# Row products and sums on VectorE for the modulation vectors of a transformer kernel, in place of matmuls

## The reference

```
sc, sc_ctx = silu(c), silu(c_ctx)                      # two vectors of 1024
for l in range(2):
    mod   = split(sc     @ w_mod[l] + b_mod[l], 6)     # w_mod[l]: 1024 x 6144
    mod_x = split(sc_ctx @ w_mod[l] + b_mod[l], 6)
    sh1, sc1, g1, sh2, sc2, g2 = mod                   # each 1024
    h = layer_norm(x) * (1 + sc1) + sh1                # context likewise, with mod_x
    x = layer_norm(ALPHA * x + g1 * mixing(h)) * ln1_g[l] + ln1_b[l]
    x = layer_norm(ALPHA * x + g2 * swiglu(layer_norm(x) * (1 + sc2) + sh2)) * ln2_g[l] + ln2_b[l]
```

## Time and profile before

| | |
|---|---|
| median of 3 runs | 3742.49 us (3740.39 to 3747.37) |
| profiled execution | 3751.51 us, span of its instructions 3749.7 us |
| mean granted TensorE clock | 0.956 |
| busy: TensorE, VectorE, ScalarE, GpSimd | 92%, 38%, 36%, 13% of the span |
| modulation weights | 96 loads of 0.5 MB out of 283.85 MB in all |

### The profile page before, as it was taken

How to read it: one execution, slowest core, us unless ns; L and a number is a source line. 1 busy time by engine, 2 the same in 40 slices (tenths; PEclk the granted TensorE clock), 3 DMA queues, 4 the chain that set the end, 5 groups by cost and what they waited for, 6 DMA issues and landing times. The chain is left out here.

```text
span 3749.7 us, 62391 instructions
## 1 busy us (share of the span) xinstructions
PE 3444.4 (92%) x26194; PEld 3168.3 (84%) x26194; DVE 1414.6 (38%) x2382; ACT 1332.8 (36%) x2368; POOL 476.7 (13%) x462
## 2 busy tenths in 40 slices
PE   6999999989999899997988888999997899959997
PEld 5999997867678899996988767999995788849997
DVE  3223333444434422334345543222224436543333
ACT  3222322345533322234246534212224437452223
POOL 1000010144400010001013201101010103100000
PEclk9999999999999999998988988999998999979998
DMA  4333222110022233331200023221212310123231
GB/s 141 113 121 128 83 76 68 58 44 29 24 68 91 90 107 123 115 108 50 63 23 24 29 79 96 63 63 62 66 60 95 129 57 24 40 85 96 91 95 52
DMA packets 81556, 283.85 MB, mean 76 GB/s; under 512 B 8768, under 2 KB 13120, under 8 KB 81152
## 3 DMA queue, kind: packets, MB, share of 16 engines
q1 hardware_dynamic: 77584, 266.96, 21.9%
q0 software_dynamic: 3264, 12.37, 1.0%
q10 hardware_dynamic: 432, 0.53, 0.0%
HBM read 277.73 MB, written 2.10 MB: 75 GB/s over the span
## 5 line engine op out<-in xcount | busy, mean ns | idle before, releaser
L1981 DVE TENSOR_TENSOR r_Wbasel<-r_Wf,r_Wbaseh 128x1024 fp32r<-128x1024 f32 (+1 forms) x269 | 339.2, 1262 | 718.8 <-ACT r_Wbaseh L1438 718.3
L1438 ACT ACTIVATE r_Wbaseh<-r_Wf 128x1024 fp32r<-128x1024 f32 (+1 forms) x269 | 279.5, 1041 | 526.8 <-PE PS L926 466.3
L924 PE MATMUL PS<-r_X1h,r_Wbaseh 128*128 128x264 f32 (+2 forms) x1216 | 391.1, 322 | 28.6 <-DVE r_RS L2329 19.1
L926 PE MATMUL PS<-r_X1h,r_Wbasel 128*128 128x264 f32 (+2 forms) x1216 | 381.3, 314 | 0.0
L925 PE MATMUL PS<-r_X1l,r_Wbaseh 128*128 128x264 f32 (+2 forms) x1216 | 381.2, 314 | 0.0
L924 PE MATMUL PS<-r_X2h,r_Wbaseh 128*128 128x256 f32 (+1 forms) x1200 | 362.1, 302 | 11.6 <-DVE r_X2l L2107 5.5
L925 PE MATMUL PS<-r_X2l,r_Wbaseh 128*128 128x256 f32 (+1 forms) x1200 | 355.8, 297 | 0.0
L926 PE MATMUL PS<-r_X2h,r_Wbasel 128*128 128x256 f32 (+1 forms) x1200 | 355.4, 296 | 0.0
L924 PEld LDWEIGHTS PS<-r_X1h,r_Wbaseh 128*128 128x128 f32 x1216 | 233.8, 192 | 59.1 <-issue 23.4
L1981 DVE TENSOR_TENSOR r_Wtopl<-r_Wf,r_Wtoph 128x1024 fp32r<-128x1024 f32 (+1 forms) x140 | 171.2, 1223 | 261.4 <-ACT r_Wtoph L1438 261.2
L924 PE MATMUL PS<-r_X2h,r_Wtoph 128*128 128x256 f32 x880 | 248.7, 283 | 9.2 <-DVE r_Wtopl L1981 9.2
(11 more groups left out here) (361 smaller groups left out, 9237.3 us busy)
## 6 DMA issues: line engine op xcount, KB each, us to landing
r_Wf<-in_wmod SPq DMA_DIRECT2D x96, 512.0 KB, 3.6
r_Wf<-in_f_in SPq DMA_DIRECT2D x88, 512.0 KB, 3.7
r_Wf<-in_g_in SPq DMA_DIRECT2D x88, 512.0 KB, 3.5
r_Wf<-in_f_out SPq DMA_DIRECT2D x32, 448.0 KB, 3.2
r_Wf<-in_g_out SPq DMA_DIRECT2D x32, 448.0 KB, 3.2
r_Wf<-in_f_out SPq DMA_DIRECT2D x16, 512.0 KB, 4.1
r_Wf<-in_w_o SPq DMA_DIRECT2D x16, 512.0 KB, 3.5
r_Wf<-in_g_out SPq DMA_DIRECT2D x16, 512.0 KB, 3.5
```

Of the source, the lines that this page charges most:

```text
L924: self.e.matmul(o, wh, xh, start=first, stop=False)
L926: return self.e.matmul(o, wl, xh, start=False, stop=last)
L1438: e.activation(p.w(i, cols)[0], p.Wf[:, i % NW, 0:cols], ACT.Copy).then_inc(*p.hi.did(i))
L1981: e.tensor_tensor(l, p.Wf[:, i % NW, 0:cols], h.bitcast(F32), ALU.subtract).then_inc(*p.lo.did(i))
```

## The change

The modulation weights are laid out transposed, so that a tile holds 128 outputs as partitions and all 1024 inputs as columns: 48 tiles of 0.5 MB a layer. `c` and `c_ctx` are loaded as rows repeated on all partitions (two loads a layer on GpSimd's queue), ScalarE takes their Silu in place (the step `rows`), and for each tile VectorE makes two scalar_tensor_tensor instructions, weights times row, whose running sum is the modulation of that partition. Biases are added for eight tiles at once. The 48 steps `mod` of layer 0 are spread over the items of f1 and those of layer 1 over f2. The groups, their matmuls, their copies and their places in the planner are gone. SyncE, which waited for TensorE to free a raw tile's buffer, waits for VectorE.

```diff
+def mod_steps(l):
+    return [("rows", l)] + [("mod", l, m) for m in range(48)]
...
-def ffn_items(f, lag, gate, groups=()):
+def ffn_items(f, lag, gate, others=()):
...
-    firsts = [i for i, x in enumerate(items) if x[0][-1] == 0 and i > 12]
-    for n in reversed(groups):
-        i = firsts[len(firsts) * (groups.index(n) + 1) // (len(groups) + 2)]
-        items.insert(i + 2, (("mturn", n), 0.9, None))
-        items.insert(i + 1, (("msum", n), 1.8, None))
-    return items
+    out, n = [], 0
+    for i, x in enumerate(items):
+        out.append(x)
+        while n < len(others) and n * (len(items) - 24) < (i - 12) * len(others):
+            out.append((others[n], 0, None))
+            n += 1
+    return out
...
-    items = [(("open", "top", []), 0, None)] + ffn_items(f, 4, lambda c: c, [1, 2, 3, 4, 5])
+    items = [(("open", "top", []), 0, None)] + ffn_items(f, 4, lambda c: c, mod_steps(0))
...
-    return woven(items, chains, [(0, -1)])
+    return woven(items, chains)
...
-    items += ffn_items(f, 4, lambda c: c, [6, 7, 8, 9, 10])
+    items.append((("vectors", 1), 0, None))
+    items += ffn_items(f, 4, lambda c: c, mod_steps(1))
...
-        return woven(items, chains, [(n, ends[0]) for n in range(11, 16)] + [(n, ends[nc]) for n in range(16, 22)])
+        return woven(items, chains)
...
-    return woven(items, chains, [(n, ends[0]) for n in (22, 23)])
+    return woven(items, chains)
...  (TensorE: mod_sum and mod_turn removed; the step "mod" only counts the tile)
+        elif what == "mod":
+            self.finished(self.get("wmod", a, 1024, True))
...  (ScalarE: mod_copy and the Silu of c at the start removed)
+        elif what == "rows":
+            l, = a
+            e.wait_ge(*p.load(("c", l)).of("in"))
+            self.logs = False
+            for c in (0, 1):
+                e.activation(p.CR[l][c], p.CR[l][c], ACT.Silu).then_inc(*p.act.did(("rows", l, c)))
...  (VectorE)
+    def modulation(self, l, m):
+        p, e = self.p, self.e
+        u = self.get("wmod", (l, m), 1024, True)
+        w = p.Wf[:, u % NW, :]
+        e.wait_ge(*p.w_arrived(u))
+        if m == 0:
+            e.wait_ge(*p.act.of(("rows", l, 1)))
+        if m or l:
+            e.wait_ge(*p.dve.of(("first", l, m - 1) if m else ("first", l - 1, 47)))
+        e.scalar_tensor_tensor(p.JK[:, :], w, 1.0, p.CR[l][0], ALU.mult, ALU.mult, p.MOD[:, l, m, 0:1]).then_inc(
+            *p.dve.did(("first", l, m)))
+        e.scalar_tensor_tensor(w, w, 1.0, p.CR[l][1], ALU.mult, ALU.mult, p.MOD[:, l, m, 1:2]).then_inc(
+            *p.dve.did(("w", u), ("sum", l, m)))
+        self.finished(u)
+        if m % 8 < 7:
+            return
...  (bias for eight tiles: one instruction, or two where 1 / ALPHA is applied)
...  (GpSimd)
+        elif what == "vectors":
+            e.wait_ge(*p.mm.of(("mixout", 7, 1)))
+            self.vectors(*a)
...
+    def vectors(self, l):
+        p, e = self.p, self.e
+        for c in (0, 1):
+            e.dma_start(p.CR[l][c], p.A["c"][:, c, :]).then_inc(*p.load(("c", l)).did("in"))
...  (GpSimd's program)
+        for i in range(4):
+            e.wait_ge(*p.x_in[i].of("x"))
+        self.vectors(0)
         e.dma_start(p.H[:, :, T1:T1 + TC], p.A["ctx"]).then_inc(*p.ctx_in.did("x"))
...  (SyncE)
             if p.order[i - NW][3]:
-                e.wait_ge(*p.mm.of(("w", i - NW)))
+                e.wait_ge(*p.dve.of(("w", i - NW)))
...  (layout of the inputs)
-    a["wmod"] = np.ascontiguousarray(i["w_mod_2"].reshape(2, 2, 4, 128, 24, 256).transpose(0, 4, 1, 3, 2, 5)).reshape(
-        2, 24, 2, 128, 1024)
+    a["wmod"] = np.ascontiguousarray(i["w_mod_2"].transpose(0, 2, 1)).reshape(2, 48, 128, 1024)
+    c = np.stack([i["c_2"].reshape(-1), i["c_ctx_2"].reshape(-1)])
+    a["c"] = np.ascontiguousarray(np.broadcast_to(c[None], (128, 2, 1024)))
```

More of the change, by code:

```diff
@@ L36 @@
 NVEC = _n
-MODS = [(l, m) for l in range(2) for m in range(24)]
 GR = ((0, 384), (384, 640), (640, 1024))
@@ L604, in chain, with woven @@
     return out
-def woven(items, chains, groups):
-    t, pos, out, turns, groups = 0.0, 0, [], [], list(groups)
+def woven(items, chains):
+    t, pos, out = 0.0, 0, []
     at = [x[2] if x[1] is None else None for x in chains]
@@ L624, in woven @@
             continue
[L625 to L628, removed]
         gate = items[pos][2] if pos < len(items) else None
@@ L637, in woven @@
             continue
[L638 to L649, removed]
+        t = min(at[j] for j in range(len(chains)) if at[j] is not None and at[j] > t)
+    return out
 def last_of(items, kind, c, n):
@@ L709, in second_sequence @@
     chains += [(chain([a], c + 1), ends[2 + c], 0.8) for c in (0, 1)]
-    return woven(items, chains, [])
+    return woven(items, chains)
 def latent_sequence(p, l):
@@ L872, in partial_sum @@
         return n % 3, self.partial[n - 3] if n >= 3 else None
[L874 to L880, removed]
     def run(self, steps):
@@ L1078, in step @@
             self.tick(*a)
[L1080 to L1106, removed]
     def quarter_sums(self, b, src, g, n):
@@ L1490, in step @@
             self.apply(*a)
-        elif what == "msum":
-            self.mod_copy(*a)
+        elif what == "rows":
[4 more added lines that the diff above has]
+                e.activation(p.CR[l][c], p.CR[l][c], ACT.Silu).then_inc(*p.act.did(("rows", l, c)))
+        elif what == "mod":
+            self.finished(self.get("wmod", a, 1024, True))
         elif what == "bar":
@@ L1953, in program @@
         e.dma_start(p.CB[:, :, :], p.A["cb"]).then_inc(*p.const_in.did("all"))
[L1954 to L1957, removed]
         self.run(p.sequences[0])
@@ L2024, in step @@
             self.apply(*a)
[L2025 to L2028, removed]
+        elif what == "mod":
+            self.modulation(*a)
         elif what == "bar":
@@ L2055, in step @@
             self.tick(*a)
-    def mod_turn(self, n):
+    def modulation(self, l, m):
         p, e = self.p, self.e
[L2059 to L2063, removed]
-                            other).then_inc(*p.dve.did(("mod", l, m)))
+        u = self.get("wmod", (l, m), 1024, True)
[12 more added lines that the diff above has]
+            return
+        x = p.MOD[:, l, m - 7:m + 1, :]
+        b0 = VEC[f"bmod{l}"][0] + m - 7
+        b = p.V[:, b0:b0 + 8].unsqueeze(2).broadcast_to([128, 8, 2])
+        e.wait_ge(*p.dve.of(("sum", l, m)))
+        if m // 8 in (2, 5):
+            e.tensor_tensor(x, x, b, ALU.add).then_inc(*p.dve.did(("biased", l, m)))
+            e.wait_ge(*p.dve.of(("biased", l, m)))
+            e.tensor_scalar(x, x, 1.0 / ALPHA, None, ALU.mult).then_inc(*p.dve.did(("mod", l, m)))
+        else:
+            e.scalar_tensor_tensor(x, x, 1.0 if m // 8 in (1, 4) else 0.0, b, ALU.add, ALU.add).then_inc(
+                *p.dve.did(("mod", l, m)))
     def newton(self, x, y, t, ready, mul, key):
@@ L2964, in put @@
         v[:, s:s + n] = arr
-    pick = np.zeros((128, 2), np.float32)
-    for c in (0, 1):
-        pick[c::32, c] = 1.0
-    put("sum", pick)
     put("eps", np.broadcast_to(np.array(EPS, np.float32), (128, 4)))
```

33 lines of the change are left out of this document (9 added, 24 removed), and 4 rows, old and new, of the table _n.

## The result

| | before | after |
|---|---|---|
| median of timed runs, same chip | 3744.86 us (3740.39 to 3747.37) | 3681.59 us (3679.88 to 3687.85) |
| ratio, 95% interval | | 0.9835, 0.9818 to 0.9852 |
| profiled execution, its span | 3751.51, 3749.7 us | 3687.85, 3686.1 us |
| busy: TensorE, VectorE, ScalarE, GpSimd | 92, 38, 36, 13% | 92, 44, 36, 13% |

The change saves 63 us; the forecast was 3671.5 us, 71 us saved, with the range 3648 to 3706. The time lies in the range and 10 us above the forecast. (2.4 of the 10 are the kernel before: with a fourth run its median is 3744.9 us, and the forecast started from 3742.5.)

What follows compares the result with a forecast made beforehand. TensorE was taken to bound f1 and f2, a chain of small steps across engines the norm stretches. Savings of 38 - 3 + 30 + 6 = 71 us from 3742.5 gave 3671.5 us, range 3648 to 3706.

Steps and rivals of the forecast that it cites:

- Removed from f1 and f2: Feed-forward parts f1 and f2: ten groups leave TensorE's queue, 2.76 us each plus idleness ahead of L1104, saving 38 us.
- Short waits: f1 and f2: added VectorE sums sometimes delay other work, charged 3 us (0 to 15).
- 12 us of buffered work: f1 and f2: four buffers hold some 12 us of work, so one freed 6 us late still comes in time.
- The instruction: VectorE in f1 and f2: each scalar_tensor_tensor with running sum takes 1.38 us, 2.76 us a tile, 132 us a layer.
- end together: Earlier trace: GpSimd's subtraction of 2.41 us and VectorE's, begun 0.9 us later, were said to end together.
- Norm stretches: Second block's three norm stretches: without groups, sums and totals run earlier, saving 11, 9 and 10 us, together 30.
- rival 2: Norm stretches give all that the groups occupy, 45 us, and the start its 9: 3650 us; chance 0.10.
- Rival 1: Norm stretches give only 8 us because the ScalarE and VectorE chain sets their end: 3693.5 us; chance 0.12.
- The start: Kernel start: squares move up, but three splits in a row hold the feed-forward tiles; saves 6 us (1 to 9).
- Rival 3: f1 and f2: running sum halves VectorE's rate, 5.2 us a tile: 3758 us; loss from 5.0 us a tile; chance 0.09.
- Rival 4: f1 and f2: each modulation tile delays TensorE 0.5 us through late weights or buffers, 48 us: 3719 us; chance 0.09.

Runs made afterwards that it cites:

- e5: Kernel before without its groups 1 to 10 (those modulations set to 0.5, their weights not loaded): 3700.2 us, ratio 0.9881.
- e2: Kernel after with both sums of each modulation tile over 8 columns in place of 1024 (modulations then wrong): 3672.4 us, ratio 0.9802.
- e3: Kernel before with all 23 later groups in f1 (12) and f2 (11), none in the norm stretches: 3775.2 us, ratio 1.0079.
- e6: Kernel after with all activations 64 bytes further up on each partition: 3664.6 us.
- e4: Kernel after with the splits of the first four weight tiles ahead of the second chunk's norm: 3676.2 us, ratio 0.9812.
- e7: Kernel after with all activations 32 bytes further up, at a multiple of 512; total time not given.
- e8: Kernel after with activations 32 bytes further up and the top weight slots 480 bytes down; total time not given, 119.2 to 119.3 ns per matmul.
- e1: Kernel after with all activations 1088 bytes further up, as before the change, and the unread product JK as bf16; total time not given.
- e10: Kernel after with each sum made twice, four instructions of 1024 columns a tile: 3861.3 us, ratio 1.0307.

## Why the prediction came out right, and where its steps did not

1. **Removed from f1 and f2, 38 us.** Mis-sized: 52 by e5. The forecast counted the pieces and ScalarE's copies around one group, behind which the clock did not fall. Behind six of the ten it did, for some 10 of the missing 14 us; the rest of what a group costs, 3.9 to 4.6 us, is near the 3.8 of the forecast.
2. **Short waits, 3 us.** Mis-sized the other way: 13 by the traces of e2, within the 0 to 15 that the forecast allowed. They were put down to VectorE's order; but VectorE was idle ahead of every split that came late, and most of the delay is the turn of the buffers, which the forecast held for covered by 12 us of buffered work. It gave the higher traffic no price either; the feed-forward weights land at 4.4 us in place of 3.7. This alone costs little, as e2 has the same 4.4. 52 - 13 = 39 and the 40 that f1 and f2 gave agree; the forecast's 35 was near because two errors met.
3. **The instruction, 1.38 us.** Right: 1.22 and 1.37. The second of a pair is longer where GpSimd works: the one that began at 1502.48 took 1.76 us while GpSimd's subtraction ran from 1501.95 to 1503.16. So did all 26 second ones that met such a subtraction already under way (1.75 to 1.78); the 70 others took 1.21 to 1.23. Where the sum had begun ahead of the subtraction, as 26 first ones of a pair did, it kept its 1.22; one first sum began behind it and took 1.41. That fits the shared port of the Trainium skill ("SBUF — State Buffer", Who interferes with whom), which gives it to one engine at a time, and is small. (The prediction read in the earlier trace rows that two subtractions "end together"; by the rows they end at 51.44 and 52.51, so VectorE's ran on by itself for 1.07 us.)
4. **Norm stretches, 30 us.** 37.7 by e3, 38.6 in the change (of which 3 us are a shift within g0, which e3 and e6, with the old places, lose there too). Between the forecast and rival 2's 45. The third alone, 10, came as forecast; the first two give 4 us more each. TensorE's queue loses 25 and 23 us of work there; how that turns into 15 and 13 us, step by step, no run takes apart. Rival 1 (8 us) is out.
5. **The start, 6 us.** 8 us. The first matmul at 38.0, as forecast, and the splits of three tiles in a row.
6. **Missing: the places.** 15 us lost in g0 and g1 by the twins of e6 (7.3 and 7.7), 17 by the medians. The diff moves every activation by 1088 bytes, and the forecast gave that no term. This is the largest thing that it lacked. With the old distance back, e6 saves 82 us in its set (3746.2 - 3664.6), 11 more than forecast; the kernel after saves 8 less. The time lay in the range because these errors met, not because each term was right: that it is so near is luck.
7. **Missing, and no part of the change: 5 us between f1 and f2.** The time from the last matmul on H1 to the first on MX, the same work in all kernels, went from 772.7 (e4) to 780.2 us (e5), 775.3 before and 779.9 after. In all thirteen traces it follows the time that the clock spends at its lower level there: 13.7 us of it in e4 and e7 (772.7 and 773.0), 20.5 before and in e6 and e8 (775.3 to 775.7), 30.7 in e3, e5 and the kernel after (779.3 to 780.2). The same 23 matmuls, once in the kernel after, once in e4, show what differs, TensorE's granted clock:

```profile
978.00:982.50 4.50, 4.43 (x23) 3.93 (x23) 0.53 (x3) 0.01 (x1) 0.00 (x0) 0.62 0.01 4
```

```profile
964.70:967.70 3.00, 2.99 (x23) 2.56 (x24) 0.51 (x2) 0.03 (x1) 0.00 (x0) 1.00 0.02 5
```

Both come behind the same 1.04 us of waiting. Why the clock falls in the one and not in the other stays open. It may well be chance of the execution and not the kernel: e1 and e6 differ by 1024 bytes in the place of the activations, which changes no pace (117.7 in g0 for both), and yet by 2.8 us here (778.5 and 775.7). The profiled execution of the kernel after was also the slowest of its four (3687.9 us), that of e2 the fastest of its four (3668.2).

Rival 2's 3650 us is out as well: its start of 9 us came as 8, its 45 of the stretches as 38, and it knew of no places. Rival 3 is out by its rate, but its sum was also too small: at the price that it named, 5.2 us a tile, e10 is 115 us slower than before, not 16. On a straight line between the two measured points at 2.6 and 5.2 us the change would break even near 3.5 us a tile (63 gained, 115 lost), an estimate from two points only, and not at 5.0. Rival 4's mechanism, weights and buffers late, is the one that is at work, with 0.13 us a tile (13 / 96) in place of its 0.5.

## What to carry to other kernels

Before costing a diff that adds or removes a tile of SBUF, write down where each operand of the hot matmuls begins before and after, modulo 1024, and compare the pace in a stretch that the change does not touch: 2 to 3% of such a stretch can hang on it. Cost work put on an idle engine by the turn of the buffer that it holds (until freed, landed, and prepared), not by the engine's busy share alone. And where a gap is taken out of a dense stretch, look at the granted clock behind several such gaps, not at one.

## What the runs showed of the hardware that was not expected

- The pace of matmuls of 256 float32 columns depends on where the stationary and the moving operand lie in SBUF against each other: 119.9 to 120.0 ns for the eight slow pairs, 116.7 to 118.7 for 23 others, 113.5 for (992, 32), at full clock with TensorE alone, on zeros. Why it is so no run tells, nor why 96 bytes beyond a multiple of 256 is as slow as a multiple.
- A gap inside a dense stretch can cost more than itself: six of ten groups were followed by 3.4 us at the lower clock level and cost 5.7 to 6.4 us, the four others 3.9 to 4.6.
- scalar_tensor_tensor on two float32 operands of 1024 columns with a running sum takes 1.22 us, as a tensor_tensor of that size, and the read of the sum 0.08 us, partly overlapped. With a GpSimd subtraction already under way it took 1.75 to 1.78 us (26 times) and 1.41 (once).
